# Encoder layer on one core: sigmoids of the first branch written into the merged activations' area, attention groups combined one token tile at a time

## What is computed

```python
wts = softmax(stack(lses), axis=0)                 # three groups, per token and head
attn = einsum('gbsh,gbshd->bshd', wts, stack(outs))
attn_branch = (attn * silu(gate_a)) @ w_br_a
hy_branch = (hy * silu(gate_h)) @ w_br_h
merged = sigmoid(g_a) * attn_branch + sigmoid(g_h) * hy_branch
out = x + rms_norm(merged @ w_out, post_g)
```

## Time and profile before

| | |
|---|---|
| median of 3 runs | 2621.7 us (2620.71 to 2631.27) |
| profiled execution | 2629.01 us, its span 2627.2 us |
| mean granted TensorE clock | 0.984 of full speed |
| PE | 2521.8 us, 96% of the span |
| PE weight load | 1542.7 us, 59% |
| DVE | 1601.2 us, 61% |
| ACT | 944.4 us, 36% |
| POOL | 477.1 us, 18% |
| DMA | 131 GB/s over the span |

### The profile page before, as it was taken

One profiled execution on the slowest core, in us unless ns is written; L12 is line 12 of the kernel. 1 busy time (PEld: TensorE's weight loads), 2 busy tenths in 40 slices (PEclk: granted clock), 3 DMA queues, 4 the chain that ended last, 5 costly groups with the idle time before them and its releaser, 6 DMA issues. The chain is left out here.

```text
span 2627.2 us, 36180 instructions
## 1 busy us (share of the span) xinstructions
PE 2521.8 (96%) x14232; PEld 1542.7 (59%) x14232; DVE 1601.2 (61%) x2279; ACT 944.4 (36%) x1901; POOL 477.1 (18%) x462
## 2 busy tenths in 40 slices
PE   6999998999999999999799999999989999999997
PEld 4444343357676767676688888656434444444586
DVE  5746656635655656565669999776773245533543
ACT  5322212235544555555543334232541113211231
POOL 0105554400000000010034453423110000000000
PEclk9999999999999999999889999999989999999999
DMA  5824535422333434343654352535431021110132
GB/s 197 302 95 158 195 149 184 173 108 99 128 133 114 144 111 153 114 167 117 229 201 161 117 188 111 194 147 197 150 118 63 32 81 33 33 33 32 57 97 81
DMA packets 145264, 341.26 MB, mean 130 GB/s; under 512 B 8137, under 2 KB 102581, under 8 KB 138056
## 3 DMA queue, kind: packets, MB, share of 16 engines
q1 hardware_dynamic: 126312, 238.94, 26.6%
q0 software_dynamic: 18640, 93.72, 9.2%
q10 hardware_dynamic: 144, 6.29, 0.7%
HBM read 215.10 MB, written 130.12 MB: 131 GB/s over the span
## 5 line engine op out<-in xcount | busy, mean ns | idle before, releaser
L1290 PE MATMUL ps<-mem 128*128 128x512 f16 (+1 forms) x9312 | 1748.3, 348 | 21.1 <-ACT mem L1673 5.3
L1290 PEld LDWEIGHTS ps<-mem 128*128 128x128 f16 x9312 | 927.7, 102 | 811.1 <-issue 75.5
L849 ACT ACTIVATE mem<-mem 128x2048 f16<-128x2048 f32 (+1 forms) x56 | 108.6, 1940 | 386.0 <-DVE mem L867 385.8
L2172 DVE TENSOR_TENSOR mem<-ps,mem 128x512 f32<-128x512 f32 (+2 forms) x144 | 79.8, 554 | 239.5 <-PE ps L1423 238.8
L1774 ACT ACTIVATE mem<-ps 128x512 f32<-128x512 f32 (+1 forms) x144 | 72.1, 500 | 311.7 <-PE ps L1436 311.3
L837 POOL PARTITION_ALL_REDUCE mem<-mem x56 | 44.1, 789 | 757.9 <-DVE mem L830 731.7
L874 DVE SCALAR_TENSOR_TENSOR mem<-mem 128x2048 f16<-128x2048 f32 (+1 forms) x56 | 132.7, 2369 | 80.4 <-ACT mem L849 80.4
L1542 PE MATMUL ps<-mem 128*128 128x256 f32 x768 | 171.4, 380 | 0.6
L1477 PE MATMUL ps<-mem 128*128 128x256 f32 (+1 forms) x640 | 168.7, 422 | 0.0
L1542 PEld LDWEIGHTS ps<-mem 128*128 128x128 f32 x768 | 144.5, 190 | 24.1 <-issue 5.5
L2207 DVE TENSOR_TENSOR mem<-mem 128x1024 f16<-128x1024 f32 x96 | 117.1, 1220 | 51.4 <-ACT mem L1795 50.9
(11 more groups left out here) (191 smaller groups left out, 2597.0 us busy)
## 6 DMA issues: line engine op xcount, KB each, us to landing
s_ks<-mem SPq DMA_DIRECT2D x96, 512.0 KB, 2.7
mem<-s_ks SPq DMA_DIRECT2D x23, 2048.0 KB, 8.7
mem<-in_w_in SPq DMA_DIRECT2D x44, 1024.0 KB, 6.2
s_sums<-mem POOLq DMA_DIRECT2D x24, 1024.0 KB, 4.3
mem<-s_sums SPq DMA_DIRECT2D x48, 512.0 KB, 3.8
s_uc<-mem POOLq DMA_DIRECT2D x24, 768.5 KB, 6.1
mem<-s_uc SPq DMA_DIRECT2D x18, 1024.0 KB, 6.6
s_og<-mem POOLq DMA_DIRECT2D x72, 132.0 KB, 2.7
```

Source lines behind the costliest of these rows:

```text
L849: act.activation(w_place(b)[:, 0, 0:chunks(b)], raw_of(b), ACT.Copy, scale=wscale[b % 3]).then_inc(S["w_hi"], 1)
L1290: mm = pe.matmul(out, lhs(a, k), rhs(b, k), start=(k == 0 and x == 0), stop=(k == kc - 1 and x == 2))
L2172: dve.tensor_tensor(l[:, :, c0:c1], ps[:, 2 + N % 2, :].rearrange("p (x c) -> p x c", x=2)[:, :, c0:c1], bias, ALU.add).then_inc(S["a_bias ...
```

## The change

- The sigmoids of this branch are written straight into `mt` (channel block d, span s), and the merge multiplies in place. They use no `sg` buffer, and ACT waits for nothing but the PE tile.
- The branch's channel blocks are taken in the order 4, 5, 6, 7, 0, 1, 2, 3. Blocks 4 to 7 of `mt` lie behind the buffers of the combining, which shrink to two `ogt`, two `cmb`, two small `wts`; `third` moves to sg[0] and sg[1].
- Twelve ma tiles instead of six are among the turns: one and two other tiles in turn behind each T (18 in all instead of 12). After the turns: ma 0, wa 4, ma 1, wa 5, 6, 7, 0, 1, ma 2, 3, wa 2, 3 (three spans each).
- Weights' order: ga, ga, ma 4-5, ma 6-7, ma 0-1, wa 4-5, wa 6-7, wa 0-1, ma 2-3, wa 2-3. In ACT's list the high half of block 4 (ma 0-1) comes when the walk reaches the first tile after the turns. `SPLITS` follows.
- Each token tile's weights are worked out alone, for one tile instead of two, in eight DVE instructions instead of twelve, with one exponential on ACT per tile. DVE waits before tile t until PE turned tile t - 2. A load of token tile t waits until tile t - 2 was combined.

```diff
-        for i in range(4):
-            M_BLOCKS += [(w_in, OFF_MG + WC * i), (w_a, WC * i)]
+        A_ORDER = (4, 5, 6, 7, 0, 1, 2, 3)
+        M_BLOCKS += [(w_in, OFF_MG + WC * i) for i in (2, 3, 0)] + [(w_a, WC * i) for i in (2, 3, 0)] + [(w_in, OFF_MG + WC), (w_a, WC)]
...
-        others = [("ga", j, 1) for j in (2, 3)] + [("ga", j, 2) for j in range(4)] + [("ma", d, s) for d in range(2) for s in range(NSP)]
+        others = [("ga", j, 1) for j in (2, 3)] + [("ga", j, 2) for j in range(4)] + [("ma", d, s) for d in A_ORDER[0:4] for s in range(NSP)]
...
-            MSEQ += [("T", x, 0)] + others[x:x + 1]
+            MSEQ += [("T", x, 0)] + others[3 * x // 2:3 * (x + 1) // 2]
+        N_TURNS = len(MSEQ)
+        for kind, d in (("ma", 0), ("wa", 4), ("ma", 1), ("wa", 5), ("wa", 6), ("wa", 7), ("wa", 0), ("wa", 1),
+                        ("ma", 2), ("ma", 3), ("wa", 2), ("wa", 3)):
+            MSEQ += [(kind, d, s) for s in range(NSP)]
...
-        SPLITS = {6 * i: (4 + 2 * i, 5 + 2 * i) for i in range(1, 5)}
+        SPLITS = {0: (6,), 3: (7,), 6: (8,), 12: (9,), 15: (10,), 18: (11,), 24: (12, 13)}
...
-                pool.dma_start(ogt[:, t % 4], og_d[:, P * t:P * t + P, :, :].rearrange("g p a c -> p g a c")).then_inc(ld_og[t // 2 % 2], 16)
+                pool.dma_start(ogt[t % 2], og_d[:, P * t:P * t + P, :, :].rearrange("g p a c -> p g a c")).then_inc(ld_og[t % 2], 16)
...
-            for t in range(4, NT):
-                pool.wait_ge(S["g_cmb"], t - 3)
+            for t in range(2, NT):
+                pool.wait_ge(S["g_cmb"], t - 1)
...
+                if n == N_TURNS:
+                    w_hi(act, M0 + 4)
+                    span_hi(2)
+                    w_hi(act, M0 + 5)
+                    act.wait_ge(S["g_cmb"], NT)
+                if kind == "wa":
+                    if s == 0:
+                        for i in SPLITS.get(NSP * A_ORDER.index(x), ()):
+                            w_hi(act, M0 + i)
                     continue
                 m_wait(act, n)
...
-                    act.activation(sg[s], ps[:, n % 8, :], ACT.Sigmoid, scale=descale[M0 + 2]).then_inc(bank_free[n % 8], 1)
+                    act.activation(mt[:, x, BANK * s:BANK * s + BANK], ps[:, n % 8, :], ACT.Sigmoid, scale=descale[block_ma(x)]
+                                   ).then_inc(bank_free[n % 8], 1)
...
+                dve.wait_ge(ld_og[t % 2], 16 * (t // 2 + 1))
+
+                chain(dve.tensor_tensor(low, nm[:, 0], nm[:, 1], ALU.min))
+                settle()
+                chain(dve.tensor_tensor(low, low, nm[:, 2], ALU.min))
+                settle()
+                dve.tensor_tensor(e, low.unsqueeze(1).to_broadcast([P, 3, 2, HH]), nm, ALU.subtract).then_inc(S["g_sc"], 1)
+                dve.wait_ge(S["g_exp"], t + 1)
+                chain(dve.tensor_tensor(ed, e, den, ALU.mult))
...
+                if t >= 2:
+                    m_wait(dve, POS["T", t - 2, 0])
...
-                    dve.scalar_tensor_tensor(mt[:, d, c], ps[:, b % 8, :], sc, sg[ns % 3], ALU.mult, ALU.mult
+                    dve.scalar_tensor_tensor(mt[:, d, c], ps[:, b % 8, :], sc, mt[:, d, c], ALU.mult, ALU.mult
```

More of the change, by code:

```diff
@@ L431, in build @@
         gated = hg_tile(KD * len(SPANS) - 1)
[L432 to L437, removed]
+        ogt = [mem[:, MERGED + i * 6 * OW:MERGED + (i + 1) * 6 * OW].rearrange("p (g a c) -> p g a c", g=3, a=2) for i in range(2)]
+        GSC = MERGED + 12 * OW
+        wts = [mem[:, GSC + 64 * i:GSC + 64 * i + 64] for i in range(2)]
+        cmb = [mem[:, GSC + 128 + 2 * AW * i:GSC + 128 + 2 * AW * (i + 1)].rearrange("p (a c) -> p a c", a=2) for i in range(2)]
+        third = sg[0:2]
         m16 = halves(mem[:, BASE:BASE + KD * T], KD, T)
@@ L717, in tile_ma @@
         def tile_ma(d, s):
[L718 removed]
+            return POS["ma", d, s]
         def tile_wa(d, s):
[L721 removed]
+            return POS["wa", d, s]
         def tile_gh(d, s):
@@ L737, in build @@
         M_DONE = [POS["ga", 2 * i + 1, NSP - 1] + 1 for i in range(2)]
-        for i in range(4):
-            M_DONE += [tile_ma(2 * i + 1, NSP - 1) + 1, tile_wa(2 * i + 1, NSP - 1) + 1]
+        M_DONE += [tile(2 * i + 1, NSP - 1) + 1 for tile, i in ((tile_ma, 2), (tile_ma, 3), (tile_ma, 0), (tile_wa, 2), (tile_wa, 3),
+                                                                (tile_wa, 0), (tile_ma, 1), (tile_wa, 1))]
         M_DONE += [tile_gh(2 * i + 1, NSP - 1) + 1 for i in range(4)]
@@ L1234, in _ @@
                             pool.wait_ge(ot_out[sl], 16 * ot_count(6 * NT - 1))
-                        for t in range(4):
-                            load_og(t)
+                        load_og(0)
+                        load_og(1)
                     c, nch = chans(i)
@@ L1599, in _ @@
             for n, (kind, x, s) in enumerate(MSEQ):
+                if kind == "wa":
+                    if x == A_ORDER[0]:
+                        pe.wait_ge(S["b_lo"], s + 1)
+                    branch_tile(n, block_wa(x), x, s, 4, lambda a, k: at16(a, s)[:, k, :])
+                    continue
                 if kind != "T":
@@ L1609, in _ @@
                 for j in range(4):
-                    mm = pe.transpose(ps[:, n % 8, P * j:P * j + P], cmb[x % 4][:, 0, P * j:P * j + P], ident)
+                    mm = pe.transpose(ps[:, n % 8, P * j:P * j + P], cmb[x % 2][:, 0, P * j:P * j + P], ident)
                 mm.then_inc(bank_ready[n % 8], 1)
[L1612 to L1618, removed]
             for s in range(NSP):
@@ L1922, in _ @@
             for n, (kind, x, s) in enumerate(MSEQ):
[L1923 to L1927, removed]
+                if n in (3, 5):
+                    combine(n // 2 - 1)
+                    weigh(n // 2 - 1)
                 if kind == "T":
@@ new lines, in _ @@
+                o, w = ogt[t % 2], wts[t % 2]
+                acc, tmp = cmb[t % 2][:, 0, :], cmb[t % 2][:, 1, :]
+                nm, den = o[:, :, :, HW:HW + HH], o[:, :, :, HW + HH:OW]
+                low, total = (w[:, c:c + 8].rearrange("p (a h) -> p a h", a=2) for c in (0, 56))
+                e, ed = (w[:, c:c + 24].rearrange("p (g a h) -> p g a h", g=3, a=2) for c in (8, 32))
+                dve.wait_ge(ld_og[t % 2], 16 * (t // 2 + 1))
+                chain(dve.tensor_tensor(low, nm[:, 0], nm[:, 1], ALU.min))
@@ new lines, in _ @@
+                settle()
[4 more added lines that the diff above has]
+                chain(dve.tensor_tensor(ed, e, den, ALU.mult))
+                settle()
+                chain(dve.tensor_tensor(total, ed[:, 0], ed[:, 1], ALU.add))
+                settle()
+                chain(dve.tensor_tensor(total, total, ed[:, 2], ALU.add))
@@ L2573, in _ @@
                     continue
-                d, s = x // NSP, x % NSP
+                d, s = AS[x] if ns < N_A else DS[x]
                 c = slice(BANK * s, BANK * s + BANK)
```

91 lines of the change are left out of this document (27 added, 64 removed).

## The result

The changed kernel takes 2606.2 us at the median of 6 runs (2599.6 to 2612.7), the kernel before 2623.6 at the median of 6 (2620.7 to 2631.3). The ratio is 0.9936, with a 95% interval from 0.9919 to 0.9953: 0.64% faster, 12 to 21 us. The forecast was 2607.7, in a range from 2602.5 to 2616.

What follows compares the result with a forecast made beforehand. PE was taken as the bound, with 23.3 us lost in gaps and slower matmuls; less 2.4, 5.3 and 1.6 that gave 14.0 us won, a median of 2607.7 us instead of 2621.7, in a range from 2602.5 to 2616.

Steps and rivals of the forecast that it cites:

- What bounds the kernel: PE, busy 96%; only 23.3 us between 1835.76 and about 2000 us can be won: gaps 15.0, slower matmuls 8.3.
- step 2: Among and behind the turns: 18 other tiles instead of 12, then ma 0; the gap of 4.19 us goes.
- Step 1: Sigmoids no longer wait for DVE to free `sg`; the gap of 1.95 us goes, at no cost.
- Step 3: Combining token tiles singly in the turns: PE waits 2.4 us at T6 and T7 together, upper bound 8.9.
- The rival of a chain that is late more often: ACT and DVE fall behind in the turns by 8.9 us, clock falls twice more: gain 4.3, 2617 us; chance 0.26.
- Step 4: Two combining buffers instead of four: DVE's waits and token tile loads cost nothing; upper bound 5.6 us.
- Step 5: PE waits 5.3 us before ma 0, as block 4's high half stands behind ma (7, 2)'s sigmoid on ACT.
- Step 6: Slower matmuls behind the new gap before ma 0 cost 1.6 us; none for T7's small gap.
- Step 7: DVE waits for copies of blocks 7 (16 us) and 11 (31 us); covered for PE, costed at nothing.
- Sum: 23.3 - 2.4 - 5.3 - 1.6 = 14.0 us won; median 2607.7 us, minus 0.53%.
- The rule against the change: Batch ACT activations by table set: a switch costs 2.66 us, not 1.30; would end slower, 2637 us, chance 0.04.

Runs made afterwards that it cites:

- e0: The changed kernel unaltered, measured again in a second comparison: 233.2 us from T0's start to the branch's last merge, ratio to before 0.9949.
- e8: Kernel before, with the last span's halves made ahead of block 4 on DVE and ACT: 247.9 us from T0 to last merge, ratio 1.0012.
- e5: e1 with wa 4 ahead of ma 0 behind the turns: 235.0 us from T0 to last merge, ratio to before 0.9968.
- e3: Changed kernel with two more table loads in each turn on ACT: 257.8 us from T0 to last merge, ratio to before 1.0032.
- e1: Changed kernel with block 4's high half ahead of the last two sigmoids on ACT: 225.0 us from T0 to last merge, ratio to before 0.9912.
- e9: Changed kernel, combining's exponential replaced by SiLU for tiles 0 to 6, then sigmoid, removing nearly all the turns' table loads: 230.5 us from T0 to last merge.
- e10: e8 plus sigmoids from d = 1 on written straight into mt: 243.3 us from T0 to last merge, ratio to before 0.9982.
- e11: Kernel before with only the sigmoids from d = 1 on written straight into mt: 241.9 us from T0 to last merge, ratio 0.9988.
- e4: Changed kernel with a sigmoid in place of combining's exponential throughout: 233.1 us from T0 to last merge.

## Why the prediction came out right, step by step

**What bounds the kernel.** Right: nothing behind the stretch moved, what moved ahead of it is scatter (e0), and the 23.3 us of loss were the whole stake. But the reading of the last two gaps as two causes side by side was wrong. e8 shows that the wait for `sg` stood behind the wait for b_lo and held PE up to about the same moment, 23.8 us behind T11 against 22.2: an earlier b_lo alone wins nothing. That the cover of step 2 alone would have won nothing here either follows from it, but was not run. The change does both, so the sum didn't suffer; that was luck, not reading.

**Step 1, sigmoids into mt.** "The gap of 1.95 goes": true, and too small. With e8 as the start the sigmoids' place and their order in ACT's list are worth 12.0 us (247.9 to 235.9).

**Step 2, cover.** The gap of 4.19 went. e5 prices the cover by ma 0 at 10.0 us.

**Step 3, combining singly.** Forecast was a delay of 2.4 us in front of T6 and T7, measured were 1.73 us, in front of T7 alone. Here is the tile as the timeline of DVE shows it, beside the earlier trace rows:

```profile
1856.79 0.16 DVE L2462 TENSOR_TENSOR mem<-mem 128x8 f32<-128x8 f32 x1
...
1857.65 0.18 DVE L2468 TENSOR_TENSOR mem<-mem 128x24 f32<-128x24 f32 x1 [0.29 <-ACT mem L1899]
...
1858.73 1.29 DVE L2482 TENSOR_TENSOR mem<-mem 128x512 f32<-128x512 f32 x2
```

and the exponentials of tiles 0, 3 and 7 in the timeline of ACT:

```profile
1842.64 0.22 ACT L1899 ACTIVATE mem<-mem 128x24 f32<-128x24 f32 x1 [0.75 <-DVE mem L2466]
...
1869.95 0.22 ACT L1899 ACTIVATE mem<-mem 128x24 f32<-128x24 f32 x1 [3.91 <-DVE mem L2466]
...
1906.04 0.22 ACT L1899 ACTIVATE mem<-mem 128x24 f32<-128x24 f32 x1 [0.88 <-DVE mem L2466]
```

A head takes 1.94 us for one tile where the prediction allowed up to 2.47 and before it was 2.47 for two. From the exponential to `weigh` it is 1.33 (1857.40 to 1858.73), less than the 1.43 assumed. The chain came out as it was added up: the seven rounds took 63.4 us (1842.64 to 1906.04) against 63.6, and ACT waited for DVE in the turns that the prediction named, 3.9, 1.3, 2.3 and 0.9 us in turns 3, 5, 6 and 7 against 4.1, 1.3, 2.1 and 1.1. A start 0.2 earlier and a tile 0.1 sooner behind its exponential make most of the rest of the 0.7. The rival of a chain that is late more often didn't come, but e3 shows how near it is: 3 us more on ACT per turn, and seven tiles are late.

**Step 4, two buffers.** As forecast: DVE never waited for a load in the turns; the twelve loads landed in 4.7 to 8.4 us, median 5.0, where a turn takes 8.2 on the mean.

**Step 5, the new wait.** Forecast 5.3 us, measured 5.12, ended by the named instruction, and gone in e1.

**Step 6, slow matmuls: the term that was mis-sized**, 1.6 us forecast, 3.3 measured. It was read off the 24 matmuls behind the gaps of 2.69 and 4.63 in the earlier trace rows. The same rows have twelve matmuls that lose 2.4 us behind the gap of 4.19 (5.11 in place of 2.7), and the loss differs from gap to gap. Busy time by stretch in the changed kernel, the last us of the gap first (the columns of the earlier trace rows):

```profile
1958.20:1959.20 1.00, 0.00 (x0) 0.00 (x0) 1.00 (x2) 0.00 (x0) 0.00 (x0) 0.59 0.00 0
1959.20:1960.20 1.00, 0.93 (x3) 0.38 (x4) 1.00 (x2) 0.00 (x0) 0.00 (x0) 0.50 0.00 0
...
1964.20:1965.20 1.00, 1.00 (x3) 0.30 (x2) 1.00 (x2) 0.00 (x0) 0.00 (x0) 0.50 0.00 0
1965.20:1966.20 1.00, 1.00 (x6) 0.49 (x5) 0.44 (x5) 0.45 (x1) 0.00 (x0) 1.00 0.00 0
```

From 1959.2 to 1965.2 the granted clock is 0.50, the level of 1.2 GHz, and a row counts 3 or 4 matmuls; then it is 1.00, and a row counts 6. Six us at half speed make three of the 3.3 lost.

**Step 7, later splits.** DVE waited 16.0 and 30.9 us for the copies of blocks 7 and 11, as laid out, and 9.3 for that of block 6; PE never waited for a block or a bank behind the start of ma 0. The low halves of blocks 7 and 11 in the timeline of DVE:

```profile
2003.07 1.28 DVE L881 SCALAR_TENSOR_TENSOR mem<-mem 128x1024 f16<-128x1024 f32 x1 [16.04 <-ACT mem L856]
...
2073.85 2.35 DVE L881 SCALAR_TENSOR_TENSOR mem<-mem 128x2048 f16<-128x2048 f32 x1 [30.93 <-ACT mem L856]
```

**Sum.** 23.3 less 6.85 and 3.3 is 13.2 against 14.0; terms 3 and 5 were 0.9 too high, term 6 1.7 too low, so a part of the agreement is two errors that cancel. The last merge was forecast near 2099 with T0 at 1866.8; it came 233.2 behind T0, which would be 2100.0. The median moved by 17.4, with an interval that holds 13.2 as well; the second comparison gave 14.0. That the median, 2606.2, lies only 1.5 from the forecast is luck: the forecast stood on a median of three runs, 2621.7, where six gave 2623.6. The whole time can't resolve what the stretch does.

**The rule against the change.** The trace agrees with the Trainium skill, "ScalarE: Activation LUTs", section "What ACT_TABLE_LOAD costs", on the load, 1.28 us, and again shows nothing of the drain. In the timeline of ACT of the changed kernel the load follows `weigh` and the next activation follows the load without a break:

```profile
1858.73 2.02 ACT L1906 ACTIVATE mem<-mem 128x64 f32<-128x64 f32 x8 [1.11 <-DVE mem L2476]
1860.76 1.28 ACT L1954 ACT_TABLE_LOAD   x1
1862.06 0.69 ACT L1954 ACTIVATE mem<-ps,mem 128x512 f32<-128x512 f32 x1
```

Its advice to batch by set is sound here all the same: without the loads (e9) 2.7 us more are won.

## What to carry to other kernels

Where engines walk fixed lists, look not only at what an instruction costs but at what it stands behind: 5.1 us here, 5.1 in e10 and 10 in e5 were the place of one to three instructions or tiles. Two gaps in a row may be one delay with two causes; estimate the second as if the first were gone, before you price either. And where whole times scatter by 10 us, compare a stretch between two instructions that both kernels have, and its pure work shows at once what is still to be had.

## What was not expected of the hardware

The same gap of 5.12 us cost 3.3 us of slow matmuls in the changed kernel and 2.3 in e9, which has no other gap; the longer gap of 8.17 us in e5 cost no more, 2.0. The rows of the granted clock show where the difference lies. In e9 the clock fell earlier in the gap than in the changed kernel, and it was back sooner behind it. Two us in e9, where PE goes on at 1963.57:

```profile
1961.57:1962.57 1.00, 0.00 (x0) 0.00 (x0) 1.00 (x1) 0.00 (x0) 0.00 (x0) 0.50 0.00 0
...
1967.57:1968.57 1.00, 1.00 (x6) 0.40 (x4) 1.00 (x1) 0.00 (x0) 0.00 (x0) 0.82 0.00 0
```

By such rows PE worked at 1.2 GHz for about 5.9 us in the changed kernel, 4.4 in e9 and 3.5 in e5, and half of that is 3.0, 2.2 and 1.7, nearly the whole loss of each. In the changed kernel the clock was still up until less than 1 us before PE went on (0.59 in the last us of the gap), in e5 it had been down for about 3.3 us. What decides when in a gap the clock falls stays open, so a gap's length alone doesn't give its price: behind gaps of 1.1 to 1.7 us nothing was lost (e1: 0.2 in all), but of two gaps of 2.6 us one cost nothing (e8, before T4) and the other 1.7 (e11, before T4).

SiLU and sigmoid needed a table load between them in e4, although neither is an exponential.
